# Delta rule: cumulative log decays by rows, in three parts, spread per pair of heads by a picked column

## The reference

```
g = -exp(a_log) * softplus(a + dt_bias)            # a log decay per token and head
gc = cumsum(g)                                     # down the tokens
diff = gc[:, None] - gc[None, :]
decay = where(tril, exp(where(tril, diff, 0)), 0)  # one matrix per head
m = where(strict, (k_beta @ k.T) * decay, 0)
t_mat = inverse(m + eye)                           # unit lower triangular
a_intra = (q @ k.T) * decay
```

## Time and profile before

| | |
|---|---|
| median of 3 runs | 1210.48 us |
| the profiled execution | 1210.57 us |
| its span | 1208.6 us |
| busy PE (TensorE matmul) | 1183.3 us, 98% |
| busy PEld (weight load) | 1069.2 us, 88% |
| busy DVE | 703.3 us, 58% |
| busy ACT | 701.7 us, 58% |
| busy POOL | 881.0 us, 73% |
| granted TensorE clock, mean | 0.997 |

### The profile page before, as it was taken

One profiled execution on the slowest core, in us unless ns is written; L12 is line 12 of the kernel. 1 busy time (PEld: TensorE's weight loads), 2 busy tenths in 40 slices (PEclk: granted clock), 3 DMA queues, 4 the chain that ended last, 5 costly groups with the idle time before them and its releaser, 6 DMA issues.

```text
span 1208.6 us, 23310 instructions
## 1 busy us (share of the span) xinstructions
PE 1183.3 (98%) x8146; PEld 1069.2 (88%) x8146; DVE 703.3 (58%) x1520; ACT 701.7 (58%) x1315; POOL 881.0 (73%) x371
## 2 busy tenths in 40 slices
PE   8999999999999999999999999999999999999996
PEld 7998898779999998889999998888798888999995
DVE  5668677456666666546666666293363525444454
ACT  7777677465555557656555656665366445444442
POOL 5847643287988987537889889888786475988882
PEclk9999999999999999999999999999999999999998
DMA  8688522256766656415566665666566344665650
GB/s 284 191 165 201 158 89 89 70 159 207 228 192 190 201 183 187 139 46 164 176 207 190 186 198 158 192 208 193 158 186 196 102 145 119 210 190 177 190 155 36
DMA packets 61354, 202.90 MB, mean 168 GB/s; under 512 B 6480, under 2 KB 13008, under 8 KB 61152
## 3 DMA queue, kind: packets, MB, share of 16 engines
q1 hardware_dynamic: 53712, 193.51, 52.3%
q10 hardware_dynamic: 7568, 8.39, 3.6%
HBM read 197.68 MB, written 4.19 MB: 167 GB/s over the span
## 4 chain that ended last, share of the span: by engine, by line
PE 70%; issue 12%; POOL 10%; DVE 5%; ACT 2%; DMA 0%; POOLq 0%; SPq 0%; DVEq 0%; ACTq 0%
PE bank L183 17%; PE bank L184 16%; PE bank L185 16%; POOL wlo L167 9%; PE solve L185 5%; PE solve L184 5%; PE solve L183 5%; DVE flo L587 1%; ACT whi L163 1%; ACT xhi L306 1%; PE bank L1771 0%; PE bank L1772 0%; DVE resid L2195 0%; PE bank L1468 0%; DVE scr L2190 0%
## 5 line engine op out<-in xcount | busy, mean ns | idle before, releaser
L167 POOL TENSOR_TENSOR wlo<-raw,whi 128x1024 fp32r<-128x1024 f32 x362 | 874.6, 2442 | 294.3 <-ACT whi L163 293.2
L163 ACT ACTIVATE whi<-raw 128x1024 fp32r<-128x1024 f32 x362 | 379.6, 1055 | 134.5 <-PE bank L185 120.0
L183 PE MATMUL bank<-xhi,whi 128*128 128x256 f32 (+1 forms) x936 | 269.8, 288 | 1.2 <-DVE xlo L312 1.0
L184 PE MATMUL bank<-xlo,whi 128*128 128x256 f32 (+1 forms) x936 | 264.6, 283 | 0.0
L185 PE MATMUL bank<-xhi,wlo 128*128 128x256 f32 (+1 forms) x936 | 264.5, 283 | 0.0
L183 PEld LDWEIGHTS bank<-xhi,whi 128*128 128x128 f32 (+1 forms) x936 | 178.3, 190 | 5.2 <-DVE xlo L312 1.3
L183 PE MATMUL bank<-whi,xhi 128*128 128x512 f32 (+2 forms) x456 | 178.2, 391 | 3.1 <-issue 2.0
L184 PEld LDWEIGHTS bank<-xlo,whi 128*128 128x128 f32 (+1 forms) x936 | 178.5, 191 | 1.1
L185 PEld LDWEIGHTS bank<-xhi,wlo 128*128 128x128 f32 (+1 forms) x936 | 178.4, 191 | 0.1
L185 PE MATMUL bank<-whi,xlo 128*128 128x512 f32 (+2 forms) x456 | 173.9, 381 | 0.0
L184 PE MATMUL bank<-wlo,xhi 128*128 128x512 f32 (+2 forms) x456 | 173.7, 381 | 0.0
(11 more groups left out here) (426 smaller groups left out, 1711.4 us busy)
## 6 DMA issues: line engine op xcount, KB each, us to landing
raw<-in_stream SPq DMA_DIRECT2D x363, 512.0 KB, 3.6
band_scratch<-band ACTq DMA_DIRECT2D x1, 3072.0 KB, 35.6
area<-band_scratch ACTq DMA_DIRECT2D x2, 1024.0 KB, 8.9
scr<-in_row_b_gate ACTq DMA_DIRECT2D x1, 1024.0 KB, 6.0
out<-resid SPq DMA_DIRECT2D x4, 256.0 KB, 2.0
tab<-in_tabs SPq DMA_DIRECT2D x1, 640.0 KB, 9.6
resid<-in_x SPq DMA_DIRECT2D x1, 512.0 KB, 3.9
resid<-in_x SPq DMA_DIRECT2D x2, 256.0 KB, 5.0
```

What stands on the lines that cost most here:

```text
L163: act.activation(whi[:, n.s, :], raw[:, n.s, :], ACT.Copy).then_inc(hi_ready, 1)
L167: pool.tensor_tensor(wlo[:, n.s, :], raw[:, n.s, :], whi[:, n.s, :].bitcast(F32), ALU.subtract).then_inc(lo_ready, 1)
L183: nc.tensor.matmul(out_ap, a_hi, b_hi, start=start, stop=False)
L184: nc.tensor.matmul(out_ap, a_hi, b_lo, start=False, stop=False)
```

## The change

A table `pick` of 16 columns is added: column c has a one in partitions c, 32 + c and 64 + c. The gates of all heads are repeated by two copies into `cosT`, for the first heads of the pairs and for the second ones as 8 equal groups of 16 columns (column 8 t + g is token block t of pair g), so that one product with `tri` gives the cumulative sums of the 16 (token block, pair) combinations as rows, each eight times over the partitions. DVE splits these rows in PSUM into three fp32r parts: partitions 0 to 31 keep the first part, 32 to 63 the second, 64 to 95 the third. In `decay_sums` the four products L897 become two of 256 columns, in which the stationary operand is a column of `pick`, repeated, and the moving one is the split rows.

```
 TABS = [...
-        ("later", 128), ("chunk_mask", 384)]
+        ("later", 128), ("chunk_mask", 384), ("pick", 16)]
...
             act.activation(fhi[:, 0, P:SEQ], tabv("future"), ACT.Copy).then_inc(GT.masks, 1)
+            act.activation(fhi[:, 2, 0:16], tabv("pick"), ACT.Copy).then_inc(GT.masks, 1)
...
-            dve.scalar_tensor_tensor(gs(G), gate_part(1), -1.0,
-                                     small[:, 16:32].unsqueeze(1).broadcast_to([P, NT, 16]), ALU.mult,
-                                     ALU.mult).then_inc(GT.g, 1)
+            dve_link(dve.scalar_tensor_tensor(gs(G), gate_part(1), -1.0,
+                                              small[:, 16:32].unsqueeze(1).broadcast_to([P, NT, 16]), ALU.mult,
+                                              ALU.mult))
+            repeat_log_decays(dve)
...
+        cum_rows, log_decays = ps[7][:, P:P + SEQ], cosT[:]
+
+        def repeat_log_decays(dve):
+            for r in range(2):
+                pairs = gsc[:, G * 32:G * 32 + 32].rearrange("p (c r) -> p r c", r=2)[:, r:r + 1, :]
+                ins = dve.tensor_copy(log_decays[:, r * P:r * P + P].rearrange("p (a c) -> p a c", a=8),
+                                      pairs.broadcast_to([P, 8, 16]))
+            ins.then_inc(GT.g, 1)
+
+        def cum_rows_split(dve):
+
+            parts = fhi[:, 1, :]
+            dve_link(dve.tensor_copy(parts, cum_rows))
+            dve_link(dve.tensor_tensor(cum_rows, cum_rows, parts.bitcast(F32), ALU.subtract))
+            dve_link(dve.tensor_copy(parts[32:64], cum_rows[32:64]))
+            dve_link(dve.tensor_copy(parts[64:128], cum_rows[64:128]))
+            dve_link(dve.tensor_tensor(cum_rows[64:128], cum_rows[64:128], parts[64:128].bitcast(F32), ALU.subtract))
+            dve.tensor_copy(parts[64:128], cum_rows[64:128]).then_inc(GT.cum_rows, 1)
...
                     pe.matmul(ps[7][:, 0:32], tri, gsc[:, G * 32:G * 32 + 32], start=True, stop=True)
+                    for r in range(2):
+                        pe.matmul(cum_rows[:, r * P:r * P + P], log_decays[:, r * P:r * P + P], tri, start=True, stop=True)
...
                     dve.tensor_scalar(gs(NGC), gs(GC), -1.0, None, ALU.mult).then_inc(GT.cum_copied, 1)
+                    cum_rows_split(dve)
...
-                pe.wait_ge(GT.masks, 2)
+                pe.wait_ge(GT.masks, 3)
+                pe.wait_ge(GT.cum_rows, 1)
             pe.matmul(bank, fhi[:, 0, 0:P], fhi[:, 0, P:SEQ].unsqueeze(1).broadcast_to([P, 4, P]), start=True, stop=False)
-            for i in range(4):
-                mm = pe.matmul(bank[:, i * P:i * P + P], scalar(G, i // 2, 2 * g + i % 2).broadcast_to([P, P]), tri,
-                               start=False, stop=i == 3)
+            for t in range(NT):
+                c = t * QKH + g
+                mm = pe.matmul(bank[:, t * SEQ:t * SEQ + SEQ], fhi[:, 2, c:c + 1].broadcast_to([P, P]), fhi[:, 1, :],
+                               start=False, stop=t == 1)
             mm.then_inc(DN.sums, 1)
...
+    t["pick"] = (i < 96) & (i % 32 == np.arange(16)[None, :])
```

More of the change, by code:

```diff
@@ L599, in build @@
         CV = sems("conv", "root bcast root_copied scaled first tap conv silu square turned copied_k")
-        GT = sems("gate", "copied ba rates exp absx logs g beta cum cum_copied masks")
+        GT = sems("gate", "copied ba rates absx logs g beta cum cum_copied cum_rows masks")
         QK, _o = carve(0, 16, SEQ)
```

## The result

| | before | after |
|---|---|---|
| median of the runs of this comparison | 1210.48 us | 1216.88 us |
| lowest to highest, 5 runs each | 1210.32 to 1211.96 us | 1215.63 to 1216.95 us |
| profiled execution, span | 1210.57, 1208.6 us | 1216.95, 1214.7 us |

The medians are 6.4 us apart; the ratio of the runs is 1.0048 (95% interval 1.0037 to 1.0059): slower, by about half a percent. The forecast was 1213.5 and its range ended at 1216.3, so the median lies 0.6 us above the range, on the side that was forecast; by the ratio (1210.48 x 1.0048 = 1216.3) the time lies on its upper end. The span of the profiled execution grew by 6.1 us, and the trace shows where.

A forecast was written before the change was run, and what follows sets the result against it. TensorE's own line was taken to bound the span until another engine makes it wait. z stage -4.0, products +0.4, split +2.6 and copies +4.0 gave +3.0 us: 1213.5 us, range 1208.8 to 1216.3.

The forecast's parts named there:

- Copies, 4.0 us: DVE after block 2: both repeated log-decay copies wait for POOL, making TensorE's turn of block 2 4.0 us late.
- the second copy slips through: After block 2: only the first copy waits for POOL, term 1.8 us, sum +0.8, 1211.3 us; chance 0.22.
- they don't meet POOL at all: After block 2: strided-source copies never wait for POOL, term 0.6 us, sum -0.4, 1210.1 us; chance 0.12.
- POOL's feed is not endangered: After block 2: POOL is several units ahead, so DVE's 4.0 us lateness would not starve it.
- Split, 2.6 us: DVE after block 11: six split instructions take 2.7 us, cover about 0.1, so TensorE stands still 2.6 us.
- Two products, 0.4 us: TensorE behind block 8: two fp32 products of 128 columns, four passes of 0.10 us, counted in full.
- z stage, -4.0 us: TensorE's z stage: 0.65 us saved per pair for pairs 2 to 7, 0.15 for pairs 0 and 1 together.
- The wait for L1038 (L1012 before) at pair 2: z stage: pair 2's product waits until DVE has used pair 0's bank, so pairs 0 and 1 give only 0.15 us.
- L866 freed: Block 11 on DVE: L866 no longer meets POOL, giving 1.6 us back; sum +1.4, 1211.9 us; chance 0.10.
- In the rest of the trace no idle is that long: Clock rival's reading: apart from the end of the run, no TensorE idle in the trace reaches the length preceding that fall.
- the rival of the clock: After the 4 us idle at 30.4 us TensorE's clock falls to 1.2 GHz: +2.3 us more, 1215.8 us; chance 0.20.
- the forecast's own scenario: Whole kernel: both copies wait and the clock stays, 1213.5 us, own range 1212.7 to 1214.3; chance 0.36.

The follow-up runs named there:

- Copies alone: Kernel before plus only the link and the two repeating copies after block 2, into a tile nobody reads: 1215.61 us, ratio 1.0044 to the kernel before.
- one copy: Changed kernel with one copy of 2x8x16 columns in place of the two of 128: 1213.59 us, ratio 1.0021 to the kernel before.

## Why the prediction was right, and where not

- **Copies, 4.0 us: right, 3.7.** Both copies waited, each for its own boundary of POOL. The size is off since POOL's instructions ended at 30.47 and 32.81 here, not at 30.7 and 33.1. Copies alone cost it (3.5 at the turn), a PSUM source takes them from 3.72 to 0.48 us, one instruction to 1.49. The Trainium skill, "SBUF — State Buffer", section "Who interferes with whom", lets the one who comes second wait for the other's whole instruction; the trace agrees, with 1.43 us to the first end and 2.37 to the next, and the strided repeated source took part, as the condition in the Trainium skill, "VectorE: DVE Perf Modes", section "What auto-detection actually checks", let one expect. The rival that the second copy slips through and the one that they don't meet POOL at all are refuted.
- **"POOL's feed is not endangered" was wrong without harm.** The kernel after shows POOL idle for 2.26 us from 32.81 on; TensorE did not wait for it.
- **Split, 2.6 us: right, 2.56 of idle,** 2.71 from turn to turn. Spread over gaps it costs nothing, which the forecast did not consider, since it took the change as it is.
- **Two products, 0.4 us: right, 0.45,** from the turn of block 5 to that of block 6. The kernel with the copies alone, which lacks the products, takes 3.46 us there, every kernel with them 3.89 to 3.91.
- **z stage, -4.0 us: right, -3.9,** and -3.8 by itself over whole runs. The repeat is 2.75 us as worked out. The wait for L1038 (L1012 before) at pair 2 came as said; the forecast's own numbers put it at 2 x 0.65 - 0.15 = 1.15 us, the trace shows 0.86 of idle.
- **L866 freed: refuted.** It still took 1.78 us, as POOL's start moved along. And with the wait taken away nothing is won once the split is gone.
- **The clock: here the forecast failed.** Its sum put the clock at nothing. I gave 0.36 to a clock that stays and 0.20 to one that falls, although the 4 us of idle that I forecast are longer than the 2.7 us that I had read between the last product and the fall at the end of the run; nothing in the working says why it should stay. It fell in every profiled execution with an idle of 3.66 us or more. The rival's price was 2.3 us; it was 1.75, since at half clock the products of 256 columns start 0.21 us apart, which is less than twice 0.12. With the copies at 3.7 that makes 1213.5 - 0.3 + 1.75 = 1215.0 us. The other 1.5 us of the profiled execution come from the v stage, a step that the forecast did not have: "In the rest of the trace no idle is that long" took it that only an idle of the length seen at the end of the run counts. The runs show falls behind 1.19 and 2.56 us as well, only not each time. With these 1.5 us and the 0.15 that split and products took beyond their terms the sum is 1216.6 us.

So the sign and four of the five places were worked out, and hold. That the time came out at the end of the range and not far beyond it is owed to the room left for the rival of the clock: the forecast's own scenario ended at 1214.3, 2.6 us below the median.

That the falls of the clock cause the time, not only go with it, is shown for block 2: with DVE's wait left as it was and TensorE kept busy, the clock stays full there, the 1.75 us to the turn of block 5 are gone and the median is 1.6 us lower. For the v stage nobody took the fall away; but the price of 1.5 us is there in each of the three profiled executions with a fall and in none of the nine without. The two of five runs of the changed kernel that took 1215.63 and 1216.03 us had a mean clock of 0.995 against 0.993 to 0.994 in the others, which fits. Why the clock falls in one execution at the v stage and not in the next stays open, and so does whether the idle of 1.19 us has a part in it.

## What to carry to other kernels

Before putting even a 128-column copy on VectorE, look at what GpSimd does at that moment and where the source lies: from PSUM the two copies took 0.48 us, from SBUF beside a busy GpSimd 3.72, the first up to the end of GpSimd's running instruction and the second up to the end of its next one. Put small steps one by one into gaps that the timeline shows ahead of a waiting instruction, not in a row; six of them went from 2.56 us to nothing. An idle of TensorE cost its length here and, where the clock fell behind it, 0.7 to 1.75 us more, so taking it away can be worth more than its length.

## What was not expected of the hardware

How often the clock fell behind an idle of TensorE, counted in the profiled executions of the twelve kernels (windows of 2 us with a granted clock below 1.00 within 4 us behind its end), for all waits of TensorE over 1.1 us from 20 us on:

| idle | place | fell |
|---|---|---|
| 3.66 to 3.83 us | turn of block 2 | 4 of 4 |
| 2.53 to 2.56 us | turn of block 11 | 3 of 5 |
| 1.43 us | turn of block 2, one copy | 0 of 1 |
| 1.24 to 1.28 us | L1468 of the kernel before, at 494.80 us | 0 of 12 |
| 1.17 to 1.19 us | v stage | 3 of 12 |
| 1.16 to 1.18 us | turn of block 1 | 0 of 9 |

The length alone doesn't order them: 1.24 to 1.28 us never had a fall behind it and 1.17 to 1.19 us had three. Each fall took 1.7 to 2.9 us of full clock by the windows, and TensorE's own timeline was late by 0.7 to 1.75 us behind it. The Trainium skill, "TensorE: Matmul & The Clock Gate", section "HAM oscillation — how this bites in real kernels", ties a return of the slow clock to idle gaps; the trace agrees for the long ones, while the three falls at the v stage came behind no more than 1.19 us. Two instructions of VectorE within SBUF, one behind the other beside a GpSimd without pause, ended with two successive instructions of GpSimd at 2, 64 and 128 columns, but not at 16 columns (1.29 and 0.17 us); width doesn't order these, and what does is open.
